# Mixer gates and branch products laid out by token, weights moving 512 columns wide, in a two-layer decoder trunk

## The reference, cut to what matters

```python
def hybrid_mixer(x, w_in, ..., w_branch, w_out):
    proj = x @ w_in
    (c_h, c_b, c_c, q, k, v, rr, rk, rv, wl, al, gl, g_conv, g_att, g_rwkv) = split_cols(proj, IN_SPLITS)
    o_conv = c_b * short_conv(c_c * c_h, conv_w)            # 512 channels
    o_att = moba_attention(rope(q), rope(k), v)             # 512 channels
    o_rwkv = rwkv7_time_mix(rr, rk, rv, wl, al, gl, ...)    # 512 channels
    p_conv, p_att, p_rwkv = jnp.split(w_branch, [512, 1024], axis=0)
    merged = (jax.nn.sigmoid(g_conv) * (o_conv @ p_conv)
              + jax.nn.sigmoid(g_att) * (o_att @ p_att)
              + jax.nn.sigmoid(g_rwkv) * (o_rwkv @ p_rwkv))
    return merged @ w_out
```

## Time and profile before

| | |
|---|---|
| three runs | 1698.21, 1699.84, 1700.64 us; median 1699.84 |
| the profiled execution | 1699.88 us, of which the trace spans 1697.9 us |
| busy in the span | PE 98%, PEld 87%, DVE 75%, ACT 59%, POOL 0% |
| mean granted TensorE clock | 0.994 of full speed |
| HBM | 241 GB/s over the span |

### The profile page before, as it was taken

One profiled execution on the slowest core, in us unless ns is written; L12 is line 12 of the kernel. 1 busy time (PEld: TensorE's weight loads), 2 busy tenths in 40 slices (PEclk: granted clock), 3 DMA queues, 4 the chain that ended last, 5 costly groups with the idle time before them and its releaser, 6 DMA issues.

```text
span 1697.9 us, 30545 instructions
## 1 busy us (share of the span) xinstructions
PE 1668.6 (98%) x12122; PEld 1482.1 (87%) x12122; DVE 1275.3 (75%) x1226; ACT 1002.4 (59%) x972; POOL 2.9 (0%) x12
## 2 busy tenths in 40 slices
PE   8999999999999999999999999999999999999997
PEld 8999899889998999989988888888888888888886
DVE  5765775565445677587468889899988889898987
ACT  5654463453344645445346776777777777777775
POOL 0000000000000000000000000000000000000000
PEclk9999999999999999999998999999999999999999
DMA  9433332566565353333266999998999989998993
GB/s 290 130 123 125 124 125 76 176 203 186 173 184 187 126 198 100 126 101 126 99 228 226 375 335 385 338 370 324 391 364 346 370 330 395 330 366 321 393 387 135
DMA packets 253058, 411.18 MB, mean 242 GB/s; under 512 B 9376, under 2 KB 134688, under 8 KB 252448
## 3 DMA queue, kind: packets, MB, share of 16 engines
q1 hardware_dynamic: 250704, 400.97, 67.2%
q10 hardware_dynamic: 2256, 8.82, 1.4%
HBM read 407.66 MB, written 2.10 MB: 241 GB/s over the span
## 4 chain that ended last, share of the span: by engine, by line
PE 87%; DVE 6%; ACT 3%; issue 2%; DMA 1%; SPq 0%; ACTq 0%; DVEq 0%
PE W L483 19%; PE W L485 18%; PE W L484 18%; PE Y L483 6%; PE Y L484 6%; PE Y L485 6%; PE Y L744 3%; ACT w_hi L1248 1%; PE W L649 1%; DVE w_lo L1742 1%; DMA raw<-w_in 1%; PE Y L649 1%; PE Y L731 1%; PE Y L1028 0%; PE Y L1029 0%
## 5 line engine op out<-in xcount | busy, mean ns | idle before, releaser
L483 PE MATMUL W<-w_lo,x_hi 128*128 128x512 f32 (+1 forms) x1120 | 390.1, 348 | 1.5 <-DVE x_lo L2054 0.9
L1742 DVE TENSOR_TENSOR w_lo<-raw,w_hi 128x2048 fp32r<-128x2048 f32 x112 | 256.6, 2292 | 173.0 <-ACT w_hi L1248 172.0
L485 PE MATMUL W<-w_hi,x_hi 128*128 128x512 f32 (+1 forms) x1120 | 385.9, 345 | 0.0
L484 PE MATMUL W<-w_hi,x_lo 128*128 128x512 f32 (+1 forms) x1120 | 385.4, 344 | 0.0
L1749 DVE TENSOR_TENSOR w_lo<-raw,w_hi 128x2048 fp32r<-128x2048 f32 x144 | 329.7, 2289 | 45.8 <-ACT w_hi L1254 45.8
L1254 ACT ACTIVATE w_hi<-raw 128x2048 fp32r<-128x2048 f32 x144 | 276.0, 1917 | 72.6 <-PE Y L485 40.1
L1749 DVE TENSOR_TENSOR w_lo<-raw_more,w_hi 128x2048 fp32r<-128x2048 f32 x120 | 274.9, 2291 | 28.3 <-ACT w_hi L1254 27.6
L483 PE MATMUL W<-x_lo,w_hi 128*128 128x256 f32 x984 | 290.0, 295 | 4.5 <-DVE w_lo L1732 4.0
L484 PE MATMUL W<-x_hi,w_lo 128*128 128x256 f32 x984 | 278.6, 283 | 0.0
L485 PE MATMUL W<-x_hi,w_hi 128*128 128x256 f32 x984 | 278.6, 283 | 0.0
L1254 ACT ACTIVATE w_hi<-raw_more 128x2048 fp32r<-128x2048 f32 x120 | 230.5, 1921 | 65.0 <-PE W L485 42.0
(11 more groups left out here) (328 smaller groups left out, 1956.7 us busy)
## 6 DMA issues: line engine op xcount, KB each, us to landing
raw<-w_in SPq DMA_DIRECT2D x123, 512.0 KB, 4.6
raw<-moe_gate SPq DMA_DIRECT2D x48, 1024.0 KB, 6.0
raw<-moe_up SPq DMA_DIRECT2D x48, 1024.0 KB, 6.7
raw<-moe_down SPq DMA_DIRECT2D x48, 1024.0 KB, 5.3
raw_more<-moe_gate SPq DMA_DIRECT2D x40, 1024.0 KB, 7.2
raw_more<-moe_up SPq DMA_DIRECT2D x40, 1024.0 KB, 6.9
raw_more<-moe_down SPq DMA_DIRECT2D x40, 1024.0 KB, 5.9
raw<-w_branch SPq DMA_DIRECT2D x24, 512.0 KB, 4.5
```

The source lines that it names most:

```text
L483: nc.tensor.matmul(out_ap, lhs[0], rhs[1], start=start, stop=False)
L484: nc.tensor.matmul(out_ap, lhs[1], rhs[0], start=False, stop=False)
L485: return nc.tensor.matmul(out_ap, lhs[0], rhs[0], start=False, stop=stop)
L1742: V.tensor_tensor(w_lo[u % 3][:], raw[u % 3][:], w_hi[u % 3][:].bitcast(F32), ALU.subtract)\
```

## The change

The gates and the branch products are computed by token: the stationary operand is 128 tokens of one channel tile of `x` or `o`, the moving operand 512 columns of the weights. A gate unit is now 512 columns by 512 input channels, so a pair of units makes one result of 256 tokens by 512 columns: both token halves accumulate in two W banks over both units of the pair (`gate_unit`), and ScalarE takes both banks out behind the second unit of the pair, with two sigmoids in a row. A unit is 24 matmuls of 512 columns. The gated sum `merged` is then by token, so it is turned by TensorE: `mturn` makes 8 transposes of 128x128 per half, 16 per layer, into the banks E and one of W, from where `msplit` splits it. The first half is turned between the two halves of branch2's second unit, the second half behind the first 24 matmuls of the output projection. In `msplit` the splits of the output weights' third and fourth unit change places with those of the sum. Two semaphores of the experts' routing (`place_done`, `counts_done`) become one, `routed`.

```diff
@@ TIMELINE
-    ("units", "branch2", 0, 1), ("msplit", 0), ("units", "branch2", 1, 2), ("msplit", 1), ("units", "out", 0, 4),
+    ("units", "branch2", 0, 1), ("front", "branch2", 1), ("mturn", 0), ("msplit", 0), ("back", "branch2", 1), ("msplit", 1),
+    ("units", "out", 0, 4),
...
@@ trunk
+        gate_rows, merged_rows = (a[:].rearrange("p k t -> p (k t)").rearrange("p (n d) -> p n d", n=NT) for a in (sgate, merged))
+
+        def turn_bank(l, q):
+            return E if q % 2 == 0 else W[(l * MIX_JOBS + JOB0["branch2"] + 1) % 3]
...
@@ sync: the loads
+                    elif kind.startswith("gate"):
+                        for q in range(n):
+                            c = where + 512 * (q // 2)
+                            load_rows(u + q, 0, w_in[l][:, c:c + 512], 512 * (q % 2), 4)
...
@@ tensor
+            def row_bank(j):
+                job_bank(j)
+                return W[j % 3][:]
...
@@ tensor: first_of_last
-                banks = [job_bank(j + h) for h in range(2)]
-
-                def product(h, m, k):
-                    c = slice((2 * h + m) * P, (2 * h + m + 1) * P)
-                    return mm3(banks[h][:, m, :], (wh[:, k, c], wl[:, k, c]), (o_hi[:, k, :], o_lo[:, k, :]), k == 0, k == BT - 1)
+                banks = [row_bank(j + t) for t in range(NT)]
+
+                def product(t, k):
+                    tk = slice(t * P, (t + 1) * P)
+                    return mm3(banks[t], (o_hi[:, k, tk], o_lo[:, k, tk]), (wh[:, k, :], wl[:, k, :]), k == 0, k == BT - 1)
...
-                for h in range(2):
-                    for k in range(BT):
-                        last = product(h, 1, k)
-                    last.then_inc(w_used if h else sem("half_done"), 1)
+                        last = product(t, k)
+                    last.then_inc(w_used if t else sem("half_done"), 1)
...
@@ tensor: branch_unit, the new gate_unit, front
-                for h in parts:
-                    bank = job_bank(j + h)
-                    for m in range(2):
-                        c = slice((2 * h + m) * P, (2 * h + m + 1) * P)
-                        for k in range(BT):
-                            last = mm3(bank[:, m, :], (wh[:, k, c], wl[:, k, c]), (o_hi[:, k, :], o_lo[:, k, :]),
-                                       k == 0, k == BT - 1)
-                    last.then_inc(w_used if h else sem("half_done"), 1)
+                for t in parts:
+                    bank, tk = row_bank(j + t), slice(t * P, (t + 1) * P)
+                    for k in range(BT):
+                        last = mm3(bank, (o_hi[:, k, tk], o_lo[:, k, tk]), (wh[:, k, :], wl[:, k, :]), k == 0, k == BT - 1)
+                    last.then_inc(w_used if t else sem("half_done"), 1)
+
+            def gate_unit(u, j, q, t):
+
+                if t == 0:
+                    unit_ready(u)
+                wh, wl = (w[u % 3][:].rearrange("p (k c) -> p k c", k=4) for w in (w_hi, w_lo))
+                bank, tk = W[(j + t) % 3][:] if q % 2 else row_bank(j + t), slice(t * P, (t + 1) * P)
+                for k in range(4):
+                    kk = 4 * (q % 2) + k
+                    last = mm3(bank, (x_hi[:, kk, tk], x_lo[:, kk, tk]), (wh[:, k, :], wl[:, k, :]), kk == 0, kk == KD - 1)
+                if t:
+                    last.then_inc(w_used, 1)
...
+                elif kind.startswith("gate"):
+                    gate_unit(u, j + 2 * (q // 2), q, part)
...
@@ tensor: mturn, and its second call in out_units
+            def mturn(l, half):
+                pe.wait_ge(sem("gated"), 8 * l + 6 + 2 * half)
+                for q in (2 * half, 2 * half + 1):
+                    if half:
+                        pe.wait_ge(sem("mlo_ready"), 4 * l + q - 1)
+                    bank = tiles(turn_bank(l, q)[:])
+                    for k in range(2):
+                        c = slice((2 * q + k) * P, (2 * q + k + 1) * P)
+                        for t in range(NT):
+                            last = transpose(bank[:, k, t * P:(t + 1) * P], merged_rows[:, t, c])
+                    last.then_inc(sem("mt_done"), 1)
...
                 out_part(l, 0, u, 1).then_inc(w_used, 1)
+                mturn(l, 1)
...
@@ scalar: out_of_bank, free_place
+                if kind.startswith("gate"):
+                    if q % 2:
+                        act.wait_ge(w_used, u + 1)
+                        for t in range(NT):
+                            b = (j - 1 + t) % 3
+                            A(gate_rows[:, t, 256 * (q - 1):256 * (q + 1)], W[b][:], ACT.Sigmoid).then_inc(bank_free[b], 1)
+                    return
...
@@ scalar: msplit
+                if half:
+                    split_hi(layer_unit(l) + UNIT0["out"] + 2)
                 for q in (2 * half, 2 * half + 1):
-                    act.wait_ge(sem("gated"), 8 * l + 4 + q + 1)
-                    c = slice(2 * q, 2 * q + 2)
-                    A(x_hi[:, c, :], merged[:, c, :], ACT.Copy).then_inc(sem("mhi_ready"), 1)
-                    if half:
-                        split_hi(layer_unit(l) + UNIT0["out"] + q)
+                    act.wait_ge(sem("mt_done"), 4 * l + q + 1)
+                    A(x_hi[:, 2 * q:2 * q + 2, :], tiles(turn_bank(l, q)[:]), ACT.Copy).then_inc(sem("mhi_ready"), 1)
                 if half == 0:
                     return
-                act.wait_ge(sem("mlo_ready"), 4 * l + 4)
-                act.wait_ge(sem("mhi_ready"), 4 * l + 4)
+                split_hi(layer_unit(l) + UNIT0["out"] + 3)
...
@@ vector: gate_half
-                ft = slice(4 * q + 2 * h, 4 * q + 2 * h + 2)
+                c = slice(512 * q, 512 * q + 512)
...
-                dst = td[:] if b else merged[:, ft, :]
-                V.tensor_tensor(dst, tiles(W[(j + h) % 3][:]), sgate[:, ft, :], ALU.mult).then_inc(free, 1)
+                gated = td[:].rearrange("p a t -> p (a t)")
+                V.tensor_tensor(gated if b else merged_rows[:, h, c], W[(j + h) % 3][:], gate_rows[:, h, c], ALU.mult).then_inc(free, 1)
...
@@ vector: msplit
+                if half:
+                    split_lo(layer_unit(l) + UNIT0["out"] + 2)
                 for q in (2 * half, 2 * half + 1):
                     dve.wait_ge(sem("mhi_ready"), 4 * l + q + 1)
                     c = slice(2 * q, 2 * q + 2)
-                    V.tensor_tensor(x_lo[:, c, :], merged[:, c, :], x_hi[:, c, :].bitcast(F32), ALU.subtract)\
+                    V.tensor_tensor(x_lo[:, c, :], tiles(turn_bank(l, q)[:]), x_hi[:, c, :].bitcast(F32), ALU.subtract)\
                         .then_inc(sem("mlo_ready"), 1)
-                    if half:
-                        split_lo(layer_unit(l) + UNIT0["out"] + q)
+                if half:
+                    split_lo(layer_unit(l) + UNIT0["out"] + 3)
```

More of the change, by code:

```diff
@@ L642, in units @@
                 elif kind.startswith("branch"):
-                    first_of_last(l, u0, j0) if a == 0 else branch_unit(l, 2, u0 + a, j0 + 2 * a)
+                    first_of_last(l, u0, j0)
+                elif kind.startswith("gate"):
+                    for q in range(a, b):
+                        front(l, kind, q)
+                        back(l, kind, q)
                 else:
@@ L1182, in last_combine @@
                             .then_inc(sem("last_comb_done"), 1)
-            handlers = {"units": units, "front": front, "back": back, "lora_w": lora_w, "lora_a": lora_a, "ss": ss,
+            handlers = {"units": units, "front": front, "back": back, "mturn": mturn, "lora_w": lora_w, "lora_a": lora_a, "ss": ss,
                         "spread": spread, "tok": tok, "scores": scores, "invert": invert, "mx": mx, "dx": dx, "cg": cg, "cu": cu,
@@ L1216, in _ @@
             nc.tensor.matmul(W[1][:, 40:48], ones, m0, start=True, stop=False)
-            nc.tensor.matmul(W[1][:, 40:48], strict, m1, start=False, stop=True).then_inc(sem("place_done"), 1)
+            nc.tensor.matmul(W[1][:, 40:48], strict, m1, start=False, stop=True).then_inc(sem("routed"), 1)
             nc.tensor.matmul(E[:, 0:NE], ones, m0, start=True, stop=False)
-            nc.tensor.matmul(E[:, 0:NE], ones, m1, start=False, stop=True).then_inc(sem("counts_done"), 1)
+            nc.tensor.matmul(E[:, 0:NE], ones, m1, start=False, stop=True).then_inc(sem("routed"), 1)
             combine = experts(MOE_U0, 0)
@@ L1256, in out_of_bank @@
             def out_of_bank(kind, q, u, j):
+                if kind.startswith("gate"):
+                    if q % 2:
+                        act.wait_ge(w_used, u + 1)
+                        for t in range(NT):
+                            b = (j - 1 + t) % 3
+                            A(gate_rows[:, t, 256 * (q - 1):256 * (q + 1)], W[b][:], ACT.Sigmoid).then_inc(bank_free[b], 1)
+                    return
                 act.wait_ge(w_used, u + 1)
                 dst = {"lora": rkvl[:, 12:14, :], "rkv": rkvl[:, 2 * RKV[q % 6]:2 * RKV[q % 6] + 2, :], "conv": share[:, 2 * q:2 * q + 2, :],
```

(11 more changed lines are left out.)

9 lines of the change are left out of this document (2 added, 7 removed).

## The result

The changed kernel takes 1704.85 us in the median of 9 runs (1702.87 to 1705.91), the kernel before 1700.01 in 9 runs beside them: ratio 1.0027, 95% interval [1.0018, 1.0035]. A second series, on another chip, gave 1703.86 against 1700.67, ratio 1.0023 [1.0013, 1.0033]. So the change costs 3 to 5 us. The forecast was 1698.9 with a range up to 1703.5.

The account below looks back on a forecast made before the run. TensorE, busy 98% of the span, was taken as the bound. Wider matmuls' 11.5 us and 1.7 of removed delays, against transposes, waits and restarts, summed to -1.0 us from 1699.9: 1698.9 us, range 1695.0 to 1703.5.

Parts of the forecast that it names:

- Wider matmuls, the gain: Gate and branch units: 24 matmuls of 512 columns replace 48 of 256, 0.32 us less per unit, 11.5 us in both layers.
- the waits behind gate1: Inversion behind gate1: the second sigmoid stands ahead of its first copy, so TensorE waits 0.6 us more a layer.
- the thinner cover: Waits on VectorE's convolution and at mx 4 grow as the halves ahead get shorter: 0.5 us a layer together.
- the clock: Rival: the granted clock falls in the waits ahead of branch2, 1.6 us each, to 1700.5 or 1702.1; chance 0.25, both 0.05.
- The wait ahead of branch2: TensorE idles until ScalarE's sigmoid frees W1: 3.0 us in layer 0, 2.3 in layer 1; 5.05 us in the sum.
- The transposes: Sixteen fp32 transposes a layer of the merged sum on TensorE cost 1.9 us, 3.8 us in all.
- The wait for `x_lo`: The output projection waits some 0.2 to 0.3 us a layer for the low part of the turned sum.
- the end of the delays for `w_lo`: Output projection's existing delays for split weights, 1.2 and 0.5 us, go because the third unit is split first.
- The short wait: Rival: ScalarE frees W1 as TensorE finishes, waits ahead of branch2 cost 1.4 us, not 5.05: 1695.2 us; chance 0.20.
- The end of the mixer: Rival: it starves, as ScalarE's and VectorE's chain runs 2 us late and each layer loses 1.6: 1703.6 us; chance 0.15.
- The wide matmuls don't save nothing: Denies the rival that a wide matmul takes as long as two narrow ones, 0.240 us: 1710.1 us; chance 0.05.

Follow-up runs that it names:

- e4_narrow: Changed kernel with every gate and branch matmul cut into two of 256 columns, part of the summing left out; 1710.79 us, ratio 1.0067 to the kernel before.
- e3_early: Changed kernel with table load and sigmoid of the last gate2 pair's first bank moved into ScalarE's earlier idle time; 1696.92 us, ratio 0.9984 to the kernel before.
- e8_look: Changed kernel run again unmodified, one execution, to look at the clock behind its two waits ahead of branch2; 1705.0 us.
- e10_longer: Changed kernel with five small sigmoids on ScalarE ahead of the pair's first sigmoid, to lengthen TensorE's waits ahead of branch2; one execution, 1704.34 us.

## Why the prediction was wrong

Two steps failed, each by 2 to 3 us, and it took both to bring the time out of the range.

**The first is "Wider matmuls, the gain", a term of the sum that was too large.** It took the pitches of the earlier trace rows, which come from streams of 24 to 96 products, for halves of 12 between small steps. "18 x 0.32" should have been 18 x 0.22: e4_narrow shows 7.9 us, half by half, for what I put at 11.5. Up to gate2's last half the forecast was -7.7 us (62 halves by 0.16, less 2.2 for the waits behind gate1 and the thinner cover); measured -5.3. The waits there were even smaller than forecast: in layer 0 they grew by 0.80 us (0.52 to 0.77 at the place of the earlier trace rows, 0 to 0.18 at mx 4, 0 to 0.37 behind gate1) where I had 1.1. The sentence "run beside splits and loads, so I take them as they are" asked the wrong question: what differs is not what runs beside the stream but how long it is. The same sentence says that both rows have the layout of the change. The narrow row doesn't: it reads `W<-o_lo,w_hi`, weights stationary. That did no harm, as e4_narrow runs narrow matmuls in the new layout 0.12 us apart too.

**The second is the clock, a term that the sum put at nothing.** I priced a fall at 1.6 us; it costs 1.4 in layer 0 and 1.6 in layer 1. But I made it a rival of 0.25 with 0.05 for both, arguing that these waits lie "in dense streams". It happens behind nine of 14 such waits. With 0.64 each the likely case was one fall and often two, and 2 us belonged into the sum; the granted clock averaged over the executions (0.9918 against 0.9939, the whole kernel taken together) says rather 3.5. The rival's rule, that the idle time has to reach the 3.04 us of the earlier trace rows, is refuted by the 2.26 of layer 1.

**What stood.** The wait ahead of branch2: 2.95 and 2.26 us where 3.0 and 2.3 were forecast, by the chain that was named. The Trainium skill (ScalarE: Activation LUTs, section What ACT_TABLE_LOAD costs) would have made it 1.4 us longer by a drain; again the trace shows none, the load ends at 316.90 and the sigmoid starts at 316.91. The transposes: 0.80 and 0.1 us a group where 0.95 was forecast. The wait for `x_lo` and the end of the delays for `w_lo` came as worked out. From gate2's last half to the mixer's end I had +6.7 us for both layers; measured 10.2, of which 3.0 are the clock, so 7.2 without.

**The sum.** -1.0 forecast, +4.9 measured in the first trace: 2.4 for the smaller gain (net of the smaller waits), 3.0 for the clock, 0.5 for the rest. Without a fall it would have been +1.9, inside the range and no measurable difference, and the error in the gain would have passed unseen.

**The rivals.** The short wait didn't come. e3_early took it away altogether and came out at 1696.9 us, near the rival's 1695.2, but that is partly luck: the rival kept 1.4 us of wait and counted on a gain that was too large. The end of the mixer doesn't starve: no wait for `w_lo` there. The wide matmuls don't save nothing; the Trainium skill's gap (TensorE: Matmul & The Clock Gate, section Back-to-back issue gap), which the page states for an isolated matmul, gives 2.5 ns for each, the runs 7.9 us / 864 = 9 ns.

## What to carry to other kernels

Price a stream by a stream of the same length that stands between the same kind of neighbours: here the difference between two pitches, taken from long streams, was 0.16 us a half, and in halves of twelve it was 0.11. When a result is drained from two buffers at the end of a stage instead of one, look whether the draining engine has an idle stretch before it, and move the table load or the first drain there; in this kernel 0.2 us of work on ScalarE was worth 6 us of the time. Put the clock into the sum of such a wait: here waits of 2.15 to 3.28 us cost their own length and, in nine of 14 cases, another 1.5 us.

## What the runs showed of the hardware

Behind an equal wait of TensorE the clock falls in one execution and not in the next. Where it falls it loses 1.7 us of full clock, or twice that (e8_look, layer 0). The fall can begin in the wait (0.82 in the window up to 318, before the restart at 317.76) or behind it. In e10_longer TensorE restarts at 317.02 and the window up to 318 still shows 1.00, the next 0.57:

```profile
316.00:318.00 2.00, 0.98 (x4) 0.86 (x5) 0.83 (x1) 2.00 (x8) 0.00 (x0) 1.00 0.96 393
318.00:320.00 2.00, 2.00 (x7) 1.54 (x6) 0.92 (x1) 1.04 (x1) 0.00 (x0) 0.57 1.04 375
```

Part of the spread of all these kernels, the one before too, is of this kind. At the head of the experts (between 892 and 924 us) the clock falls in all 14 traces; seven of them lose 3.4 us of full clock there and seven 5.1, two and three times 1.7.
